# A streaming encoder layer on one core: the gate columns move into the index keys' weight tile, and the attention logits are fused with their row maximum

## The chip, the cores and the metric

The kernel runs on one core of one Trainium2 chip. A core has a matrix engine (TensorE, PE in the profile; its weight loads are shown as PEld), a vector engine (VectorE, DVE), a scalar engine (ScalarE, ACT), a general engine (GpSimd, POOL) and a queue that issues DMAs (SyncE, SP). The metric is the device time of one execution in microseconds; less is better.

## The reference, cut to what matters

One layer of a hybrid encoder is computed for 1024 prompt tokens and 8 x 16 sample tokens, 1152 in all, in float32: a half-step feed-forward block, a token mixer, a second feed-forward block, and a final norm. The change lies in the mixer:

```python
aq, ak, av, iq, ik, iw, mq, mk, mv, mif, mo, gates = jnp.split(h @ w_in, offs, axis=-1)
...
rel = jax.nn.relu(jnp.einsum('bqhd,bsd->bqhs', q_idx, k_idx))
score = jnp.einsum('bqhs,bqh->bqs', rel, w_idx) * IDX_SCALE       # 4 index heads
_, sel = lax.top_k(score, top_k)
...
logits = (jnp.einsum('bqhd,bqkd->bqhk', q, k_sel) * DH_A ** -0.5
          - alibi_slopes()[None, None, :, None] * dist[:, :, None, :])
p = jax.nn.softmax(logits, axis=-1)                               # 8 heads, 64 wide
```

`w_in` is 1024 x 4556. Its columns are, in order: 512 attention queries, 64 + 64 keys and values, 256 index queries, 64 index keys, 4 index weights, 1024 columns of mLSTM queries, keys and values, 8 mLSTM gates (`mif`), 512 output gates (`mo`), 2048 branch gates.

## The kernel before

The program is a row of phases with a barrier after each: `load_residual`, `ffn`, `project`, `prepare_mix`, `mlstm`, `mlstm_output`, `attention`, `output`, `ffn`, `final_norm`. Activations lie transposed, channels on the 128 partitions and tokens along the free dimension. Every float32 product is made of three in a reduced-precision format (`product3`): operands are split into a high part (ScalarE copies it) and a low part (GpSimd subtracts), and TensorE adds low x high, high x low and high x high.

**`project`** (`d_` tiles) multiplies the normed activations with `w_in` in tiles of 128 columns. A tile is 3 groups of 384 tokens x 8 blocks of 128 channels x 3 products, 72 matmuls of 384 columns. The list `COLS` gives the first nine tiles: two of index queries, one with index keys and index weights (`C_IK`, tile 2), four of attention queries, one of keys and values, and one that begins at the eight gate columns (`C_MI`, tile 8, `GATES`). Then come 8 tiles of mLSTM columns, which stay on chip (`mix`), and 20 that ScalarE puts through a sigmoid into `stage`, from where they are stored to DRAM. That is 37 tiles. `HEAD` is unrolled, `LOOP1` and `LOOP2` are hardware loops over two tiles each. For each tile `load` issues the DMA on SyncE, `split_hi` (ScalarE) and `split_lo` (GpSimd) make `d_w_hi` and `d_w_lo`, `unit` (TensorE) multiplies, `evict` (ScalarE) empties PSUM, `store` (SyncE) stores. Weight buffers are double (`n0 % 2`), and `load` runs one tile ahead.

Between tile 2 and tile 3 every engine runs `scores`: SyncE issues `copies()` (the index keys doubled to both halves of the partitions, six DMAs that count up `dup`, and others), ScalarE and VectorE split queries and keys, TensorE makes the index scores. Then VectorE runs the top-k selection alone (`max` and `match_replace` in turn), while TensorE goes on with tile 3 and the rest. The selection leaves in `DM`, for each query and key, the distance to the key, plus 1e30 where the key is not selected. The gates' tile is stored whole to DRAM (`sc_v[N_SIG]`), and `prepare_mix` reads its eight rows back.

**`attention`** (`t_` tiles) runs 52 items over 9 query tiles of 128 rows; query tile t sees (t + 1) x 128 keys, the sample tile 528. An item is 4 heads for the first two query tiles, 2 for the next two, and 1 for the rest. For an item i, TensorE makes `product(i)` into `t_ps_l`; VectorE makes `logits(i)` with one instruction for each head (distance x slope + product), one `reduce_max` over the item and one small multiply that gives the negated maximum `t_nm`; ScalarE's `probs(i)` takes the exponential with the row sum; VectorE's `normalise(i)` multiplies with the inverse sum; TensorE's `transposes(i)` turn the probabilities, ScalarE's `evict(i)` copies them, TensorE's `values(i)` multiply them with the values. The order of each engine's queue is written by hand. TensorE's is:

```python
                product(0)
                product(1)
                for i in range(len(ITEMS)):
                    if i + 2 < len(ITEMS):
                        product(i + 2)
                    transposes(i)
                    ...
                    if i:
                        values(i - 1)
```

and VectorE's is `logits(0)`, `logits(1)`, then `normalise(i)`, `logits(i + 2)` for each i. The queries of query tile t + 2 are split by ScalarE (`query_hi`) and GpSimd (`query_lo`) after the last item of query tile t.

Of the kernel before, what the change touches and what calls it, by code (L numbers as in the profile page):

```python
# [22 lines left out]
P = 128  # L23
# [12 lines left out]
HA = 8  # L36
# [14 lines left out]
SLOPE = [2.0 ** (-8.0 * (h + 1) / HA) / QK_SCALE for h in range(HA)]  # L51
# [18 lines left out]
def constants():  # L70
# [7 lines left out]
    c["slope"] = -np.repeat(np.array(SLOPE, np.float32), DEC_SEQ)[:, None]  # L78
# [490 lines left out]
def project(nc, ctx, M, K, io, out, xT, x_dram, xn_hi, xn_lo, aq, kvT, DM, mix, aq_at, kvT_at, mix_at, scratch):  # L569
# [13 lines left out]
    COLS = [C_IQ, C_IQ + P, C_IK, C_AQ, C_AQ + P, C_AQ + 2 * P, C_AQ + 3 * P, C_AK, C_MI]  # L583
    HEAD, LOOP1, MID, LOOP2, TAIL = range(9), (9, N_MIX // 2 - 1), range(15, 19), (19, N_SIG // 2 - 2), (35, 36)
    GATES, MIX, SIG = 8, 9, 17
    TILES = [7, 6, 5, 4, 3, 2, NTP]
    with ExitStack() as mem, M.scope():
# [18 lines left out]
        pair_mask = M.high("pair_mask_sb", [P, 4, P])  # L606
        k_lo = M.at("d_k_lo", [P, SEQ], M.low_end, F32R)
# [52 lines left out]
        with nc.Block() as block:  # L660
            @block.sync
            def _(sp):
                def load(i, n0):
                    if n0 >= 2:
                        sp.wait_ge(lo_ok, i * 2 + (n0 - 1))
                    if n0 < len(COLS):
                        src = w_v[:, :, COLS[n0]:COLS[n0] + P]
                    elif n0 < SIG:
                        src = w_v[:, :, bass.ds(i * (2 * P) + (C_MQ + (n0 - 9) * P), P)]
                    else:  # L670
                        src = w_v[:, :, bass.ds(i * (2 * P) + (C_MO + (n0 - 17) * P), P)]
                    sp.dma_start(raw[:, n0 % 2], src).then_inc(w_in[n0 % 2], 16)

                def store(i, n0):
                    if n0 != GATES and n0 < SIG:
                        return
                    sp.wait_ge(ev_ok, i * (2 * NCH) + NCH * (n0 + 1))
                    if n0 == GATES:
                        sp.dma_start(sc_v[N_SIG], stage[:, 0]).then_inc(gates_out, 16)
                        return  # L680
# [5 lines left out]
                def copies():  # L686
                    sp.wait_ge(ev_ok, 3 * NCH)
                    for half in range(2):
# [13 lines left out]
                def first():  # L702
# [4 lines left out]
                    for dst, n in ((dist_p, "dist_p"), (dist_s, "dist_s"), (pair_mask, "pair_mask")):  # L707
# [8 lines left out]
            def _(act):  # L716
                def split_hi(i, n0):
                    act.wait_ge(w_in[n0 % 2], i * 16 + 16 * (n0 // 2 + 1))
# [4 lines left out]
                def evict(i, n0):  # L723
                    if n0 == 3:
                        act.wait_ge(spilled, 16)
                    if n0 == MIX:
                        act.wait_ge(acc_ok, len(TILES) * NI)
                    if n0 == SIG:
# [3 lines left out]
                    for c in range(NCH):  # L732
# [15 lines left out]
                        nc.scalar.activation(dst, src, ACT.Sigmoid if n0 >= SIG else ACT.Copy)\  # L748
# [39 lines left out]
            def _(pe):  # L788
# [15 lines left out]
                def scores():  # L804
                    pe.wait_ge(ld, 16 * (DEC_BATCH + 3))
# [692 lines left out]
def attention(nc, ctx, M, K, io, E, DM, o_hi, o_lo):  # L1498
# [17 lines left out]
    with ExitStack() as mem, M.scope():  # L1516
# [9 lines left out]
        mx, nm, sm, inv = (M.low("t_" + n, [P, 2, 4]) for n in ("mx", "nm", "sm", "inv"))  # L1526
# [675 lines left out]
```

## Time and profile before

| what | value |
|---|---|
| median of 3 runs | 2839.64 us (2838.19 to 2847.57) |
| the profiled execution's own time | 2833.4 us |
| its span, first to last instruction | 2831.4 us |
| TensorE, VectorE, GpSimd, ScalarE busy | 95%, 42%, 26%, 25% of the span |
| mean granted TensorE clock | 0.965 |
| `project` | about 861 to 1407 us of the span |
| `attention` | about 1556 to 1753 us |

Times in the views are microseconds from the start of the span, unless marked ns. An engine counts as busy while an instruction runs on it; the number in brackets behind a timeline row is how long the engine was idle before it, and what ended that. Matmuls are pipelined, so the ends of matmuls overlap with the next starts: starts are the better measure. A few matmul records are missing from a trace.

### The profile page before, as it was taken

To read this page: it belongs to the slowest core of one execution; us is meant where nothing else is said; L and a number is where in the kernel's file an instruction comes from. 1 tells how busy PE (TensorE), PEld (TensorE's weight loads), DVE (VectorE), ACT (ScalarE), POOL (GpSimd) and SP (SyncE) were. 2 spreads that over 40 slices of the span, in tenths; PEclk is the share of its full clock that TensorE was granted. 3 is DMA by queue.
4 is the path that set the end of the run, shared out by engine and by line. 5 is a ranking of instruction groups with operands and counts; after the bars stand their busy time and mean duration, and the time that the engine had idled before them with its cause. 6 is when DMAs were issued, how large, how long until landed. Compare 5 with 4: busy or idle time off the path is not lost. (4 is left out here: it accounts for less than half of the span.)

```text
span 2831.4 us, 38415 instructions
## 1 busy us (share of the span) xinstructions
PE 2694.5 (95%) x15459; PEld 2605.1 (92%) x15459; DVE 1198.0 (42%) x2109; ACT 700.8 (25%) x1258; POOL 726.6 (26%) x396
## 2 busy tenths in 40 slices
PE   7999999999998899999886898998999999999998
PEld 7999999999997599999864686998999999999998
DVE  5122222222234699999644785423222222222226
ACT  5111111111124311211163774112311111111112
POOL 5222222222214012111221311422522222222221
PEclk9999999999999899999976899998999999999999
DMA  4111111111103111132312201331111111111101
GB/s 129 44 45 45 45 45 33 43 45 45 45 1 127 39 46 45 55 95 90 86 41 51 46 1 57 122 135 45 53 45 45 31 45 45 45 45 42 33 30 75
DMA packets 193642, 154.50 MB, mean 55 GB/s; under 512 B 32292, under 2 KB 178128, under 8 KB 193244
## 3 DMA queue, kind: packets, MB, share of 16 engines
q1 hardware_dynamic: 193500, 152.45, 18.2%
q8 instruction: 109, 1.79, 0.3%
q14 instruction: 33, 0.27, 0.0%
HBM read 124.56 MB, written 23.90 MB: 52 GB/s over the span
## 5 line engine op out<-in xcount | busy, mean ns | idle before, releaser
L356 PE MATMUL f1ps_up<-xn_lo,f1w_hi 128*128 128x384 f32 x1056 | 354.3, 335 | 8.3 <-POOL xn_lo L311 8.3
L356 PE MATMUL f2ps_up<-xn_lo,f2w_hi 128*128 128x384 f32 x1056 | 354.0, 335 | 5.3 <-POOL xn_lo L311 5.2
L357 PE MATMUL f1ps_up<-xn_hi,f1w_lo 128*128 128x384 f32 x1056 | 353.8, 335 | 0.0
L358 PE MATMUL f1ps_up<-xn_hi,f1w_hi 128*128 128x384 f32 x1056 | 353.7, 335 | 0.0
L357 PE MATMUL f2ps_up<-xn_hi,f2w_lo 128*128 128x384 f32 x1056 | 353.3, 335 | 0.0
L358 PE MATMUL f2ps_up<-xn_hi,f2w_hi 128*128 128x384 f32 x1056 | 353.3, 335 | 0.0
L356 PE MATMUL d_ps<-xn_lo,d_w_hi 128*128 128x384 f32 x888 | 299.3, 337 | 7.5 <-POOL xn_lo L311 5.8
L357 PE MATMUL d_ps<-xn_hi,d_w_lo 128*128 128x384 f32 x888 | 298.1, 336 | 0.0
L358 PE MATMUL d_ps<-xn_hi,d_w_hi 128*128 128x384 f32 x888 | 298.0, 336 | 0.0
L514 DVE TENSOR_TENSOR f1hid<-f1gate,f1ps_up 128x384 f32<-128x384 f32 x66 | 36.6, 554 | 503.2 <-ACT f1gate L483 503.2
L514 DVE TENSOR_TENSOR f2hid<-f2gate,f2ps_up 128x384 f32<-128x384 f32 x66 | 36.6, 554 | 503.1 <-ACT f2gate L483 503.1
L435 POOL TENSOR_TENSOR f2w_lo<-f2raw,f2w_hi 128x2048 fp32r<-128x2048 f32 x33 | 152.1, 4608 | 217.7 <-ACT f2w_hi L431 217.7
L356 PEld LDWEIGHTS f1ps_up<-xn_lo,f1w_hi 128*128 128x128 f32 x1056 | 199.0, 188 | 9.7 <-issue 9.4
L783 POOL TENSOR_TENSOR d_w_lo<-d_raw,d_w_hi 128x1024 fp32r<-128x1024 f32 x37 | 89.1, 2408 | 459.7 <-ACT d_w_hi L721 459.6
L435 POOL TENSOR_TENSOR f1w_lo<-f1raw,f1w_hi 128x2048 fp32r<-128x2048 f32 x33 | 152.0, 4607 | 213.2 <-ACT f1w_hi L431 213.2
L356 PEld LDWEIGHTS f2ps_up<-xn_lo,f2w_hi 128*128 128x128 f32 x1056 | 198.7, 188 | 6.9 <-issue 6.7
L357 PEld LDWEIGHTS f1ps_up<-xn_hi,f1w_lo 128*128 128x128 f32 x1056 | 199.1, 189 | 0.1
L358 PEld LDWEIGHTS f1ps_up<-xn_hi,f1w_hi 128*128 128x128 f32 x1056 | 199.1, 188 | 0.0
L357 PEld LDWEIGHTS f2ps_up<-xn_hi,f2w_lo 128*128 128x128 f32 x1056 | 198.8, 188 | 0.1
L358 PEld LDWEIGHTS f2ps_up<-xn_hi,f2w_hi 128*128 128x128 f32 x1056 | 198.6, 188 | 0.0
L522 DVE SCALAR_TENSOR_TENSOR xT<-f2ps_dn,xT 128x384 f32<-128x384 f32 x264 | 147.2, 558 | 113.7 <-PE f2ps_dn L358 113.4
L522 DVE SCALAR_TENSOR_TENSOR xT<-f1ps_dn,xT 128x384 f32<-128x384 f32 x264 | 147.2, 558 | 113.7 <-PE f1ps_dn L358 113.4
(302 smaller groups left out, 5402.5 us busy)
## 6 DMA issues: line engine op xcount, KB each, us to landing
f1raw<-in_w_ffn_up SPq DMA_DIRECT2D x44, 512.0 KB
f2raw<-in_w_ffn_up SPq DMA_DIRECT2D x44, 512.0 KB
d_raw<-in_w_in SPq DMA_DIRECT2D x37, 512.0 KB, 4.1
p_dram<-stage SPq DMA_DIRECT2D x21, 576.0 KB, 3.1
f1raw<-in_w_ffn_down SPq DMA_DIRECT2D x11, 1024.0 KB
f2raw<-in_w_ffn_down SPq DMA_DIRECT2D x11, 1024.0 KB
b_sg<-p_dram SPq DMA_DIRECT2D x16, 576.0 KB, 4.9
x_dram<-xT SPq DMA_DIRECT2D x1, 4608.0 KB, 15.1
```

The source lines that it names most:

```text
L356: nc.tensor.matmul(out, w_hi, x_lo, start=first, stop=False)
L357: nc.tensor.matmul(out, w_lo, x_hi, start=False, stop=False)
L358: return nc.tensor.matmul(out, w_hi, x_hi, start=False, stop=final)
L435: nc.gpsimd.tensor_tensor(slot(w_lo, n0), slot(raw, n0), slot(w_hi, n0).bitcast(F32), ALU.subtract).then_inc(lo_ok, 1)
L514: nc.vector.tensor_tensor(hid[:, q0 % 2], gate[:, q0 % 2], ps_up[:, c, 1, 0:CH], ALU.mult).then_inc(hid_ok, 1)
L522: nc.vector.scalar_tensor_tensor(x, ps_dn[:, r % 2, 0:CH], 0.5, x, ALU.mult, ALU.add).then_inc(dn_ev, 1)
L783: nc.gpsimd.tensor_tensor(w_lo[:, n0 % 2], raw[:, n0 % 2], w_hi[:, n0 % 2].bitcast(F32), ALU.subtract).then_inc(lo_ok, 1)
```

## The change

Two edits. First, the gates' tile is gone: `COLS` has eight entries, and tile 2 (`INDEX`) is loaded by two DMAs, 96 columns from the index keys on and 32 columns from the gates on, so that the gates come out in rows 96 to 103 of `ikw`. They are stored from there, in front of the copies of the index keys; ScalarE's wait for that store is now at the first `mix` tile. 36 tiles are left, and all tile numbers behind the eighth move down by one. Second, ScalarE's eviction of the attention queries scales them by -1/8 / slope of their head (`qscale`, a new constant that is loaded with the others), so that (distance + product) x slope is the negated logit; one tensor_tensor_reduce for each head writes it together with its minimum over the keys, which is `t_nm`. The reduce over the item, the small multiply and two semaphores go; the exponential takes scale -1.

```diff
-SLOPE = [2.0 ** (-8.0 * (h + 1) / HA) / QK_SCALE for h in range(HA)]
+SLOPE = [2.0 ** (-8.0 * (h + 1) / HA) for h in range(HA)]
...
-    c["slope"] = -np.repeat(np.array(SLOPE, np.float32), DEC_SEQ)[:, None]
+    c["slope"] = np.repeat(np.array(SLOPE, np.float32), DEC_SEQ)[:, None]
+    c["qscale"] = -QK_SCALE / np.repeat(np.array(SLOPE, np.float32).reshape(4, 2).T, DH, axis=0)
...
-    COLS = [C_IQ, C_IQ + P, C_IK, C_AQ, C_AQ + P, C_AQ + 2 * P, C_AQ + 3 * P, C_AK, C_MI]
-    HEAD, LOOP1, MID, LOOP2, TAIL = range(9), (9, N_MIX // 2 - 1), range(15, 19), (19, N_SIG // 2 - 2), (35, 36)
-    GATES, MIX, SIG = 8, 9, 17
+    COLS = [C_IQ, C_IQ + P, C_IK, C_AQ, C_AQ + P, C_AQ + 2 * P, C_AQ + 3 * P, C_AK]
+    HEAD, LOOP1, MID, LOOP2, TAIL = range(8), (8, N_MIX // 2 - 1), range(14, 18), (18, N_SIG // 2 - 2), (34, 35)
+    INDEX, MIX, SIG, G_ROW = 2, 8, 16, 96
...
                 def load(i, n0):
                     if n0 >= 2:
                         sp.wait_ge(lo_ok, i * 2 + (n0 - 1))
+                    if n0 == INDEX:
+                        sp.dma_start(raw[:, 0, :, 0:G_ROW], w_v[:, :, C_IK:C_IK + G_ROW]).then_inc(w_in[0], 16)
+                        sp.dma_start(raw[:, 0, :, G_ROW:P], w_v[:, :, C_MI:C_MI + P - G_ROW]).then_inc(w_in[0], 16)
+                        return
...
                     sp.wait_ge(ev_ok, i * (2 * NCH) + NCH * (n0 + 1))
-                    if n0 == GATES:
-                        sp.dma_start(sc_v[N_SIG], stage[:, 0]).then_inc(gates_out, 16)
-                        return
...
                 def copies():
                     sp.wait_ge(ev_ok, 3 * NCH)
+                    sp.dma_start(sc_v[N_SIG, 0:2 * HM], ikw[G_ROW:G_ROW + 2 * HM, :]).then_inc(gates_out, 16)
...
-                    for dst, n in ((dist_p, "dist_p"), (dist_s, "dist_s"), (pair_mask, "pair_mask")):
+                    for dst, n in ((dist_p, "dist_p"), (dist_s, "dist_s"), (pair_mask, "pair_mask"),
+                                   (qscale, "qscale")):
...
-                    act.wait_ge(w_in[n0 % 2], i * 16 + 16 * (n0 // 2 + 1))
+                    act.wait_ge(w_in[n0 % 2], i * 16 + 16 * (n0 // 2 + 1 + (n0 >= INDEX and n0 % 2 == 0)))
...
                     if n0 == 3:
                         act.wait_ge(spilled, 16)
+                        act.wait_ge(ld, 16 * (DEC_BATCH + 4))
                     if n0 == MIX:
                         act.wait_ge(acc_ok, len(TILES) * NI)
-                    if n0 == SIG:
                         act.wait_ge(gates_out, 16)
...
-                        nc.scalar.activation(dst, src, ACT.Sigmoid if n0 >= SIG else ACT.Copy)\
+                        nc.scalar.activation(dst, src, ACT.Sigmoid if n0 >= SIG else ACT.Copy,
+                                             scale=qscale[:, n0 - 3:n0 - 2] if 3 <= n0 < 7 else 1.0)\
                             .then_inc(ev_ok, 1)
...
-                    pe.wait_ge(ld, 16 * (DEC_BATCH + 3))
+                    pe.wait_ge(ld, 16 * (DEC_BATCH + 4))
...
                         if t < NTP:
-                            dist, by = DM[:, SCORE_OFF[t]:SCORE_OFF[t] + L], -SLOPE[x]
+                            dist, by = DM[:, SCORE_OFF[t]:SCORE_OFF[t] + L], SLOPE[x]
...
-                        last = v.scalar_tensor_tensor(heads(lg, i)[:, y], dist, by, ps_l[:, i % 2, base:base + L],
-                                                      ALU.mult, ALU.add)
+                        last = v.tensor_tensor_reduce(heads(lg, i)[:, y], dist, ps_l[:, i % 2, base:base + L], by,
+                                                      -TAKEN, ALU.add, ALU.min, nm[:, i % 2, y:y + 1])
                     last.then_inc(lg_ok, 1)
-                    dve.wait_ge(lg_ok, i + 1)
-                    v.reduce_max(mx[:, i % 2, 0:g], heads(lg, i), AX_X).then_inc(mx_ok, 1)
-                    dve.wait_ge(mx_ok, i + 1)
-                    v.tensor_scalar(nm[:, i % 2, 0:g], mx[:, i % 2, 0:g], -QK_SCALE, None, ALU.mult)\
-                        .then_inc(nm_ok, 1)
...
-                    act.wait_ge(nm_ok, i + 1)
+                    act.wait_ge(lg_ok, i + 1)
...
-                                                    bias=nm[:, i % 2, y:y + 1], scale=QK_SCALE,
+                                                    bias=nm[:, i % 2, y:y + 1], scale=-1.0,
```

## Rows read from the trace of the kernel before

**Rows 1.** The page, busy time of each engine.
```profile
PE 2694.5 (95%) x15459; PEld 2605.1 (92%) x15459; DVE 1198.0 (42%) x2109; ACT 700.8 (25%) x1258; POOL 726.6 (26%) x396
```

**Rows 2.** Windows, tiles 3 to 36: PE, PEld, DVE, ACT, POOL busy, clock, DMA share, GB/s.
```profile
978.70:1402.80 424.10, 424.10 (x2448) 424.10 (x2448) 393.25 (x649) 82.94 (x136) 79.56 (x33) 1.00 0.22 67
```

**Rows 3.** Timeline (start, duration), both ends of the projection behind the scores.
```profile
978.57 0.42 PE L356 MATMUL d_ps<-xn_lo,d_w_hi 128*128 128x384 f32 x1
...
1385.37 2.79 DVE L930 TENSOR_TENSOR DM<-DM,dist_s_sb 128x528 f32<-128x528 f32 x1
...
1402.81 0.34 PE L358 MATMUL d_ps<-xn_hi,d_w_hi 128*128 128x384 f32 x1
1406.91 2.16 PE L1124 MATMUL e_ps<-ident_sb,kvT 128*128 128x128 f32 x9 [3.76 <-PEq L660]
```

**Rows 4.** DMA issues from 855 to 960: count, KB each, median us to landing.
```profile
d_raw<-in_w_in SPq DMA_DIRECT2D x6, 512.0 KB, 4.8
iqm<-in_cache_idx_k SPq DMA_DIRECT2D x8, 128.0 KB, 5.2
```

**Rows 5.** Timeline, the head of the projection.
```profile
880.61 1.05 SPq L672 DMA_DIRECT2D d_raw<-in_w_in  x2
...
890.79 4.91 POOL L783 TENSOR_TENSOR d_w_lo<-d_raw,d_w_hi 128x1024 fp32r<-128x1024 f32 x2
...
892.17 1.05 ACT L721 ACTIVATE d_w_hi<-d_raw 128x1024 fp32r<-128x1024 f32 x1
...
906.38 1.05 ACT L721 ACTIVATE d_w_hi<-d_raw 128x1024 fp32r<-128x1024 f32 x1
...
925.51 1.06 ACT L763 ACTIVATE d_k_hi<-ikd 128x1024 fp32r<-128x1024 f32 x1 [4.72 <-DMA iqd<-iq]
...
929.51 1.22 DVE L879 TENSOR_TENSOR d_k_lo<-ikd,d_k_hi 128x1024 fp32r<-128x1024 f32 x1
```

**Rows 6.** Windows, the attention's query tile with 1024 keys; columns as in rows 2.
```profile
1686.80:1717.80 31.00, 30.81 (x217) 25.27 (x215) 27.85 (x41) 20.62 (x40) 2.32 (x3) 1.00 0.01 1
```

**Rows 7.** Groups by form, attention, VectorE: busy us, mean ns, idle before.
```profile
L1701 DVE SCALAR_TENSOR_TENSOR t_lg<-DM,t_ps_l 128x1024 f32<-128x1024 f32 x8 | 9.8, 1221 | 2.6 <-PE t_ps_l L1632 2.5
L1705 DVE TENSOR_REDUCE t_mx<-t_lg 128x1 f32<-128x1024 f32 x8 | 9.8, 1220 | 0.3
...
L1701 DVE SCALAR_TENSOR_TENSOR t_lg<-DM,t_ps_l 128x128 f32<-128x128 f32 x8 | 1.8, 281 | 4.7 <-PE t_ps_l L1632 4.7
```

**Rows 8.** Groups by line, attention, VectorE; shapes of a line taken together.
```profile
L1705 DVE TENSOR_REDUCE t_mx<-t_lg 128x1 f32<-128x640 f32 (+8 forms) x52 | 50.8, 976 | 1.8
...
L1707 DVE TENSOR_SCALAR t_nm<-t_mx 128x1 f32<-128x1 f32 (+2 forms) x52 | 8.7, 166 | 1.8
```

**Rows 9.** Waits of TensorE, 1577.5 to 1751: us in total, times, longest.
```profile
PE t_ps_t L1647 <- DVE t_p L1719: 2.7, 6, 0.8
PE t_ps_t L1647 <- DVE t_p L1717: 0.7, 3, 0.3
...
PEld t_ps_t L1647 <- DVE t_p L1719: 4.9, 7, 1.2
PEld t_ps_t L1647 <- DVE t_p L1717: 4.4, 16, 0.6
```

**Rows 10.** Timeline, TensorE, two items: 512 keys, then 1024 keys.
```profile
1605.40 0.40 PE L1632 MATMUL t_ps_l<-t_k_lo,t_qs 128*128 128x512 f32 x1
1606.60 1.09 PE L1647 MATMUL t_ps_t<-ident_sb,t_p 128*128 128x128 f32 x8 [0.79 <-DVE t_p L1719]
...
1713.28 0.39 PE L1632 MATMUL t_ps_l<-t_k_lo,t_qs 128*128 128x512 f32 x1
1713.51 1.03 PE L1647 MATMUL t_ps_t<-ident_sb,t_p 128*128 128x128 f32 x8
```

**Rows 11.** Timeline, from the second item's normalisation to the third query tile.
```profile
1570.40 0.69 DVE L1719 TENSOR_TENSOR t_p<-t_p,t_inv 128x512 f32<-128x512 f32 x1
...
1577.81 0.66 PE L1631 MATMUL t_ps_l<-t_k_hi,t_qs 128*128 128x384 f32 x1 [4.99 <-POOL t_qs L1590]
```

More of the change, by code:

```diff
@@ L606, in project @@
         pair_mask = M.high("pair_mask_sb", [P, 4, P])
+        qscale = M.low("qscale", [P, 4])
         k_lo = M.at("d_k_lo", [P, SEQ], M.low_end, F32R)
@@ L668, in load @@
                     elif n0 < SIG:
-                        src = w_v[:, :, bass.ds(i * (2 * P) + (C_MQ + (n0 - 9) * P), P)]
+                        src = w_v[:, :, bass.ds(i * (2 * P) + (C_MQ + (n0 - MIX) * P), P)]
                     else:
-                        src = w_v[:, :, bass.ds(i * (2 * P) + (C_MO + (n0 - 17) * P), P)]
+                        src = w_v[:, :, bass.ds(i * (2 * P) + (C_MO + (n0 - SIG) * P), P)]
                     sp.dma_start(raw[:, n0 % 2], src).then_inc(w_in[n0 % 2], 16)
                 def store(i, n0):
-                    if n0 != GATES and n0 < SIG:
+                    if n0 < SIG:
                         return
                     sp.wait_ge(ev_ok, i * (2 * NCH) + NCH * (n0 + 1))
-                    if n0 == GATES:
-                        sp.dma_start(sc_v[N_SIG], stage[:, 0]).then_inc(gates_out, 16)
-                        return
                     tile = i * 2 + (n0 - SIG)
@@ L1525, in attention @@
         k_lo = M.at("t_k_lo", [P, SEQ], E["kvT_at"], F32R)
-        mx, nm, sm, inv = (M.low("t_" + n, [P, 2, 4]) for n in ("mx", "nm", "sm", "inv"))
+        nm, sm, inv = (M.low("t_" + n, [P, 2, 4]) for n in ("nm", "sm", "inv"))
         ofs = M.low("t_ofs", [P, 2, 2 * P])
@@ L1530, in attention @@
         ps_o = psum(nc, mem, "t_ps_o", [P, HA, P])
-        (ld, ldm, qk, lg_ok, mx_ok, nm_ok, p_ok, inv_ok, pn_ok, tr, tr_ev, pv, of_ok, hi, lo,
+        (ld, ldm, qk, lg_ok, p_ok, inv_ok, pn_ok, tr, tr_ev, pv, of_ok, hi, lo,
          kh_ok, kl_ok, qh_ok, ql_ok) = (
-            sem(n) for n in ("ld", "ldm", "qk", "lg_ok", "mx_ok", "nm_ok", "p_ok", "inv_ok", "pn_ok", "tr",
+            sem(n) for n in ("ld", "ldm", "qk", "lg_ok", "p_ok", "inv_ok", "pn_ok", "tr",
                              "tr_ev", "pv", "of_ok", "hi", "lo", "kh_ok", "kl_ok", "qh_ok", "ql_ok"))
```

## The prediction

> **What bounds the kernel now.** I read the page first for the share of each engine: TensorE is busy 2694.5 us of a span of 2831.4 us, 95%, and VectorE, the next one, 42% [rows 1]. That is only an average, so I went on to the two stages that the change touches and asked in each which wait ends last.
>
> The first stage is the projection. After the indexer's scores TensorE runs its remaining 34 weight tiles without a gap: the window from 978.7 to 1402.8 has 424.10 us of TensorE busy in 424.10 us, at a granted clock of 1.00, while VectorE, which does the top-k selection meanwhile, is busy 393.25 us [rows 2]. The timeline gives the two ends: the first matmul starts at 978.57, the last at 1402.81, and the next phase starts at 1406.91, when the last eviction, its store and the barrier are through [rows 3]. VectorE's last instruction of the phase ends at 1385.37 + 2.79 = 1388.16 [rows 3]. So TensorE sets the end of this stage, and VectorE is 14.6 us earlier.
>
> The second stage is the attention (1561 to 1751). With 1024 keys TensorE is busy 30.81 of 31.00 us and VectorE 27.85 [rows 6]. Each engine waits for the other in turn, and since TensorE's queue is in order, the time that counts is what TensorE loses in front of its transposes, where it waits for the normalised probabilities `t_p` of VectorE [rows 9].
>
> **The change, part by part. The weight tile.** The eight gate columns no longer have a tile of their own. A tile is 3 column groups x 8 blocks x 3 products = 72 matmuls. From rows 3: (1402.81 - 978.57) / (34 x 72 - 1) = 0.1733 us from start to start, so a tile is 72 x 0.1733 = 12.48 us. The loops keep their lengths (3, 8 bodies of two tiles); one unrolled tile of the head goes. Gone with it are a 512 KB load, its ScalarE split and its GpSimd split, three evictions and a 576 KB store, all of which ran beside the matmuls: I count them at nothing, since TensorE has no gap there that they could have filled [rows 2]. The sum of this part is -12.5 us, if the stage stays TensorE's.
>
> Does it? The last matmul then starts at 1390.3, and the next phase could start at 1406.91 - 12.48 = 1394.4. VectorE's selection does not depend on the tiles behind the scores and ends at 1388.16 as before: its margin shrinks from 18.7 to 6.2 us. It is not used up unless the selection starts over 6 us late. What could delay it lies in front of the scores, and is the next part.
>
> **Packing and the moved store.** Tile 2 is now loaded in two pieces, 96 and 32 columns, so 384 and 128 bytes per row instead of 512, twice as many pieces (2048). The issue is the second of two at 880.61, so about 881.1; ScalarE splits that tile at 892.17; at 906.38 ScalarE splits tile 3, for which it waits until tile 1 is multiplied, so TensorE begins tile 2 at about 906.3 [rows 5]. Bounds for the landing: 4.8 us, as the whole tiles of that stretch, or four times the 5.2 us of a key cache load, which has 512 pieces of 256 bytes [rows 4], so 20.8 us. At the low end nothing moves. At the high end the tile lands at 902, its splits take 1.05 us on ScalarE and 2.4 on GpSimd [rows 5], and it is there at 905.4, still before 906.3. I take the low end, and 0 us; being later than that would cost its lateness one for one. The constant `qscale` (2 KB) adds one short issue in front of the load of tile 1, hidden by the same margin, and TensorE's wait for one more load at the scores is long met. The gate store is now issued from the index keys' tile in front of the six copies that feed `d_k_hi`: one issue more, bounded by 0 and 0.6 us (two issues took 1.05 us [rows 5]). ScalarE starts `d_k_hi` at 925.51, so it ends at 926.6, but VectorE takes up `d_k_lo` only at 929.51 because of its own queue [rows 5]: 2.9 us of cover, so 0. The load of tile 4 behind them is needed only after 978. ScalarE's wait for the constants in front of tile 3 lies behind the scores and is met; behind it in its queue are only evictions. The scale of the query eviction becomes an operand of an instruction that was there.
>
> **The fused logits.** 72 scalar_tensor_tensor instructions become 72 tensor_tensor_reduce, and 52 reduces and 52 small multiplies go: 50.8 + 8.7 = 59.5 us of VectorE [rows 8], among them two waits of VectorE on itself per item. The trace has no such fused instruction. Nearest are the unfused one on the same operands, 1221 ns for 1024 columns and 281 ns for 128, thus (1221 - 281) / 896 = 1.049 ns a column and 147 ns fixed, and the reduce at 1220 ns [rows 7]. Lower bound: as the unfused one. Upper bound: both in a row, 2.44 us, two passes, which leaves VectorE where it was. I take one pass plus a readout of the row minimum like the small multiply, at most 166 ns [rows 8], because both present instructions run at the same rate for a column.
>
> The Trainium skill (VectorE: DVE Perf Modes, section Two Vector instructions with no wait between them) has it that an instruction which also writes out its accumulator is two, the main one and a read of the accumulator; no row of VectorE shows this here, and it would not change the sum.
>
> What is that worth? VectorE's removed time is not the gain; TensorE's lost time is. Where nothing holds it, a transpose starts 0.23 us after the last 512-column matmul (1713.28 to 1713.51); in the fourth query tile it is 1.20 us (1605.40 to 1606.60), thus 0.97 lost [rows 10]. Reading all 48 items from the third query tile on in this way gives 0.9 us in the third, 2.8 in the fourth, 1.8 in the next four and 0.5 in the sample tile: 6.0 us. The waits' view bounds it: 2.7 + 0.7 = 3.4 us by matmuls, 4.9 + 4.4 = 9.3 by weight loads [rows 9]. Without the reduce VectorE needs about 1.3 us less per item at 1024 keys, far more than is lost anywhere, so most of it should go; TensorE is next, and ScalarE's exponentials and copies, which stand in one queue, may keep some. I take 4.6 of the 6.0.
>
> In front of that TensorE waits for the third tile's query split, which hangs on VectorE: item 1's normalisation starts at 1570.40, then come its transposes, their eviction, the query's two splits, and the product at 1577.81 [rows 11]. Three items' logits lie before 1570.40. The first saves nothing (item 1's product is only just ready). The second saves a reduce of 512 columns (147 + 512 x 1.049 = 684 ns) and 0.17, the third 1.22 and 0.17, together 2.2 us; eight readouts at some 0.1 us, since small instructions overlap, take back 0.8. That leaves 1.4 us (0 to 2.2).
>
> **Sum.** -12.5 - 4.6 - 1.4 = -18.5 us. The profiled execution took 2833.4 us itself (its span and 2.0 around it) and would take 2814.9. The median of the runs shown is 2839.64, 6.2 us above it; the same difference gives 2821.1.
>
> **Rivals.** *A, the tile alone pays:* the fused instruction needs two passes, and VectorE keeps its load; attention gains at most 1 us. For it: no row shows the fused instruction. Against it: the unfused one reads the same two operands at 1.049 ns a column. -12.5 - 0.5 = -13 gives 2826.6. The Trainium skill (Vector Engine (DVE) Microarchitecture Reference, section Points that are easy to get wrong) says that a two-source instruction with accumulation and two non-bf16 SBUF sources runs at half throughput. Here one source is PSUM; should it hold all the same, it is this rival. Chance 0.14.
>
> *B, the head or the selection holds the tile's gain back:* tile 2 lands late, or the selection slips by over 6.2 us. A wait of x us at tile 2 moves scores, selection and end by x. It would have to land over 906.3 - 881.1 - 3.4 = 21.8 us after its issue, more than four times what the whole tiles take [rows 4]. With 5 us lost: -13.5, 2826; with 10 lost, 2831. The Trainium skill (DMA: Bandwidth & Descriptors, section Specifications) wants at least 512 B per transfer for full rate, so by it the pieces are slower; at half rate, by an estimate, they land within 10 us, hidden. Chance 0.05.
>
> *C, slower than before:* the fused instruction streams at several passes. All items have 8 x 4608 + 8 x 528 = 41088 columns, so each further pass costs 41088 x 1.049 ns = 43.1 us of VectorE, against 59.5 removed. In the tile of 1024 keys two further passes cost 2 x 8.6 us, the reduces and multiplies give back 11.0, and 3.1 us idle [rows 6] absorb half of the rest: 3 us longer in 31. That tile has a fifth of all columns, and the others have more idle time, so attention would be some 10 us longer, and the total -2.5, no change. It turns slower just beyond three passes; at four, 10 + 43 us longer in attention, -12.5 + 53 gives 2880. Against it: no two-source row is slower than one pass. Chance 0.03.
>
> *D, more gain:* all 9.3 us of the weight loads' waits and 2.2 at the start go: -24, 2815.6. Chance 0.04. The forecast, with a gain of 15 to 23, has 0.74.
>
> **Range and chances.** 2815 to 2829: D's end below, A's above with some 2 us for the median of a few runs that lie 9 us apart. For the forecast alone 2816.5 to 2825. A measurement of this kernel can tell about 0.3%, 8.5 us, from no change. Forecast, A, D and half of B are faster by more: 0.93. Same 0.04 (the other half of B, and C near three passes). Slower 0.03.
>
> **What the profile after should show.** 2592 instead of 2664 matmuls on `d_ps`, 36 weight splits; from the last score to the last matmul 33 x 12.48 = 411.8 us without a gap; the weight load of tile 2 landing before 892; VectorE's selection ending about 6 us before the next phase begins; the fused row at 1.2 to 1.4 us for 1024 columns and no reduce; VectorE in the 1024-key tile about 18 instead of 28 us busy of some 31; waits of the transposes for `t_p` near 1 us; the third tile's first product about 1.4 us nearer to the phase's first. The forecast is wrong if the fused row is over 2 us, if TensorE's gap before the transposes moves to ScalarE or to another place of its queue, or if TensorE waits at tile 2.

## The result, and the profile after

The kernel with the change takes 2820.76 us (median of 5 runs, 2818.27 to 2823.03) beside 2839.64 us (5 runs) for the kernel before: ratio 0.9936, 95% interval 0.992 to 0.9952, 18.9 us less. 2821.1 was forecast. The profiled execution took 2819.09 us itself, with a span of 2817.3 us, 14.1 less than that of before; the forecast for it was 2814.9. So the median agrees while the profile misses 4.2 us, and the parts have to be taken one at a time.

The page's busy times; [rows 1] are those of before:

```profile
PE 2683.2 (95%) x15387; PEld 2597.3 (92%) x15387; DVE 1138.7 (40%) x2077; ACT 696.5 (25%) x1254; POOL 721.3 (26%) x395
```

VectorE has 59.3 us less work and TensorE 72 matmuls fewer. The 59.5 counted for VectorE are met partly by chance: in the attention its busy time falls by 57.5 us (154.0 to 96.6), for the row minima are now read out by an instruction of their own, and 2.1 us come from one add at the end of the selection, seen below. The timeline of both ends of the projection behind the scores, beside [rows 3]:

```profile
979.47 0.42 PE L357 MATMUL d_ps<-xn_lo,d_w_hi 128*128 128x384 f32 x1
...
1386.25 0.71 DVE L936 TENSOR_TENSOR DM<-DM,dist_s_sb 128x528 f32<-128x528 f32 x1
...
1394.39 0.33 PE L359 MATMUL d_ps<-xn_hi,d_w_hi 128*128 128x384 f32 x1
...
1398.59 2.15 PE L1130 MATMUL e_ps<-ident_sb,kvT 128*128 128x128 f32 x9 [3.87 <-PEq L662]
```

The next phase starts 8.3 us earlier, not 12.5. The selection ends at 1386.96 and leaves 11.6 us, so it is not what holds the stage. From the first matmul to the last are 414.92 us for 33 tiles, 0.1747 us a matmul instead of 0.1733. Windows of 300 us of before, then of after (columns as in [rows 2]):

```profile
1000.00:1300.00 300.00, 300.00 (x1732) 300.00 (x1731) 289.66 (x438) 59.61 (x98) 57.69 (x24) 1.00 0.21 63
```

```profile
1000.00:1300.00 300.00, 300.00 (x1719) 300.00 (x1719) 289.70 (x438) 59.05 (x96) 55.35 (x23) 1.00 0.21 63
```

Both are busy all the time at a granted clock of 1.00, and still one does 1732 matmuls and the other 1719. A busy share can't show this; the count can.

The DMA issues of the head, from 855 to 925, and the timeline of the queue:

```profile
d_raw<-in_w_in SPq DMA_DIRECT2D x1, 384.0 KB, 5.6
...
d_raw<-in_w_in SPq DMA_DIRECT2D x1, 128.0 KB, 6.2
```

```profile
880.51 0.74 SPq L669 DMA_DIRECT2D d_raw<-in_w_in  x1
881.29 2.98 SPq L670 DMA_DIRECT2D d_raw<-in_w_in  x1
...
891.17 1.05 ACT L726 ACTIVATE d_w_hi<-d_raw 128x1024 fp32r<-128x1024 f32 x1
```

Tile 2's second piece lands at 881.29 + 6.2 = 887.5, before the 892 that was asked for, and ScalarE splits it without a wait.

VectorE in the attention, by form, beside [rows 7] and [rows 8]:

```profile
L1707 DVE CUSTOM_DVE_ANT_0 t_lg<-DM,t_ps_l 128x1024 f32<-128x1024 f32 x8 | 9.8, 1222 | 13.4 <-PE t_ps_l L1638 13.4
...
L1707 DVE DVE_READ_ACCUMULATOR2_ANT t_nm<- 128x1 f32 x72 | 5.9, 83 | 0.0
...
L1707 DVE CUSTOM_DVE_ANT_0 t_lg<-DM,t_ps_l 128x128 f32<-128x128 f32 x8 | 1.8, 284 | 5.5 <-PE t_ps_l L1638 5.5
```

The fused instruction takes 1222 ns for 1024 columns, the unfused one took 1221: one pass. The row minimum comes out in an instruction of its own of 83 ns. The Trainium skill (VectorE: DVE Perf Modes, section Two Vector instructions with no wait between them) says that such an instruction is two, and these rows agree. TensorE's waits, 1567 to 1735, beside [rows 9]:

```profile
PE t_ps_t L1653 <- DVE t_p L1720: 0.6, 1, 0.6
```

```profile
PEld t_ps_t L1653 <- DVE t_p L1720: 1.1, 1, 1.1
...
PEld t_ps_t L1653 <- DVE t_p L1718: 0.2, 1, 0.2
```

What was 3.4 us in 9 waits of the matmuls is 0.6 us in one. In the windows, a stretch of 31 us at the tile of 1024 keys shows VectorE at 16.40 us, where it was 27.85 in [rows 6]:

```profile
1669.50:1700.50 31.00, 31.00 (x221) 26.10 (x219) 16.40 (x32) 20.48 (x40) 1.97 (x3) 1.00 0.01 1
```

Last, the start of the attention in the timeline, beside [rows 11]: first product, item 1's normalisation, GpSimd's split, third query tile, and the phase's last values:

```profile
1552.22 0.45 PE L1637 MATMUL t_ps_l<-t_k_hi,t_qs 128*128 128x128 f32 x1 [8.79 <-POOL t_qs L1596]
...
1559.29 0.69 DVE L1720 TENSOR_TENSOR t_p<-t_p,t_inv 128x512 f32<-128x512 f32 x1
...
1563.27 2.65 POOL L1596 TENSOR_TENSOR t_qs<-aq,t_qs 64x512 fp32r<-64x512 f32 x2 [8.43 <-ACT t_qs L1777]
...
1566.06 0.66 PE L1637 MATMUL t_ps_l<-t_k_hi,t_qs 128*128 128x384 f32 x1 [3.65 <-POOL t_qs L1596]
...
1733.28 0.43 PE L1673 MATMUL t_ps_o<-t_pt,vn 16*64 16x128 f32 x2
```

The third tile starts 13.84 us behind the first product; before it was 1577.81 - 1561.10 = 16.71. From the first product to the last values are 181.06 us; before, with these rows, 189.28:

```profile
1561.10 0.44 PE L1631 MATMUL t_ps_l<-t_k_hi,t_qs 128*128 128x128 f32 x1 [8.80 <-POOL t_qs L1590]
...
1573.99 1.22 DVE L1719 TENSOR_TENSOR t_p<-t_p,t_inv 128x1024 f32<-128x1024 f32 x1
1574.12 3.54 POOL L1590 TENSOR_TENSOR t_qs<-aq,t_qs 64x512 fp32r<-64x512 f32 x2 [10.42 <-ACT t_qs L1776]
...
1750.38 0.43 PE L1667 MATMUL t_ps_o<-t_pt,vn 16*64 16x128 f32 x2
```

The open points: why the matmuls are slower, why the attention gives 8.2 us and not 6.0, and where the profile's remaining 8.3 + 8.2 - 14.1 = 2.4 us went (the span is only 14.1 us shorter).

### The profile page after: what moved, and what is told of

Read it like the earlier page. It is cut to its first block and busy times, and to the rows that moved or that the text cites. A ratio compares the mean times of both kernels' runs of the same rounds, so it can differ in the third digit from the quotient of the medians.

```text
span 2817.3 us, 38246 instructions
## 1 busy us (share of the span) xinstructions
PE 2683.2 (95%) x15387; PEld 2597.3 (92%) x15387; DVE 1138.7 (40%) x2077; ACT 696.5 (25%) x1254; POOL 721.3 (26%) x395
## 5 line engine op out<-in xcount | busy, mean ns | idle before, releaser
L357 PE MATMUL d_ps<-xn_lo,d_w_hi 128*128 128x384 f32 x864 | 293.1, 339 | 6.3 <-POOL xn_lo L312 4.7
L358 PE MATMUL d_ps<-xn_hi,d_w_lo 128*128 128x384 f32 x864 | 291.8, 338 | 0.0
L359 PE MATMUL d_ps<-xn_hi,d_w_hi 128*128 128x384 f32 x864 | 291.6, 338 | 0.0
L436 POOL TENSOR_TENSOR f2w_lo<-f2raw,f2w_hi 128x2048 fp32r<-128x2048 f32 x33 | 152.1, 4608 | 217.8 <-ACT f2w_hi L432 217.8
L436 POOL TENSOR_TENSOR f1w_lo<-f1raw,f1w_hi 128x2048 fp32r<-128x2048 f32 x33 | 152.0, 4606 | 212.9 <-ACT f1w_hi L432 212.9
```

The lines of the kernel that those rows point to most:

```text
L357: nc.tensor.matmul(out, w_hi, x_lo, start=first, stop=False)
L358: nc.tensor.matmul(out, w_lo, x_hi, start=False, stop=False)
L359: return nc.tensor.matmul(out, w_hi, x_hi, start=False, stop=final)
L436: nc.gpsimd.tensor_tensor(slot(w_lo, n0), slot(raw, n0), slot(w_hi, n0).bitcast(F32), ALU.subtract).then_inc(lo_ok, 1)
```

## The experiments

*Tiles* is the time from the first to the last start of a projection matmul behind the scores, *attention* that from the first product to the last values, and *clock* TensorE's mean granted clock in the 10 us from the third query tile's first product on.

**The two parts alone, and both kernels again.** The first two are the change without the one part or without the other:

```diff
 # e1_tile_only: the logits as before
+                        last = v.scalar_tensor_tensor(heads(lg, i)[:, y], dist, by, ps_l[:, i % 2, base:base + L],
+                                                      ALU.mult, ALU.add)
...
+                    v.reduce_max(mx[:, i % 2, 0:g], heads(lg, i), AX_X).then_inc(mx_ok, 1)
 # e2_fuse_only: the tiles as before
+    COLS = [C_IQ, C_IQ + P, C_IK, C_AQ, C_AQ + P, C_AQ + 2 * P, C_AQ + 3 * P, C_AK, C_MI]
```

> The packed tile alone: 36 weight tiles, logits and maximum as before. By the prediction the projection gives 12.5 us and nothing else moves, so about 2827 on the median. The rival from the profile after is that the shorter kernel runs its projection matmuls 0.8% slower (0.1747 us from start to start instead of 0.1733): then the phase behind the projection starts only 8 to 9 us earlier, about 2831. The start-to-start time of the matmuls behind the scores decides: 0.1733 or 0.1747.

> The fused logits alone: 37 weight tiles as before. By the prediction the attention gives 6.0 us (4.6 in front of the transposes, 1.4 at its start), about 2833.6 on the median. By the profile after it gives 8.2 us between the first product and the last values (2.9 of them at the start), about 2831.4. The matmuls of the projection should keep 0.1733 us from start to start if the slower rate belongs to the packed tile; if they show 0.1747 here as well, the rate belongs to the execution and not to the change.

> The changed kernel once more, nothing edited. If the slower matmul rate belongs to the kernel, the 33 tiles behind the scores take 415 us again (0.1747 us from start to start). If it belongs to the execution, another value comes out, 0.1733 as likely as any. Attention from first product to last values 181.1 us again, within 0.3.

> The kernel before once more, nothing edited. If its rate belongs to the kernel, the 34 tiles behind the scores take 424.2 us again (0.1733 us from start to start); if it varies from execution to execution, up to 427.6 (0.1747). Attention from first product to last values 189.3 us again, within 0.3.

Measured: e1 2828.56 us beside 2837.99 (ratio 0.9967, 0.9953 to 0.9981), e2 2830.47 (0.997, 0.9953 to 0.9986). The tile alone gives 9.4 us and the fused logits 7.5, about the whole together. In the profiles:

| kernel | tiles | us a matmul | attention | clock |
|---|---|---|---|---|
| before; e4, the same | 424.24; 424.23 (34) | 0.1733 | 189.28; 189.22 | 0.85; 0.86 |
| after | 414.92 (33) | 0.1747 | 181.06 | 0.73 |
| e3, as after | 419.67 (33) | 0.1767 | 179.84 | 0.85 |
| e1, tile only | 414.93 (33) | 0.1747 | 190.32 | 0.69 |
| e2, fused only | 432.39 (34) | 0.1767 | 180.99 | 0.74 |

The same program has 0.1747 in one execution and 0.1767 in the next, and e2, with its 37 tiles, has 0.1767. So the packed tile is not needed for the slow rate. The spread of the attention has another source, the last column. Before the third tile TensorE stands idle, for 5.0 us with the old logits and for 3.6 to 4.2 with the new, and around the tile's start its granted clock falls to the lower of its two levels. In some executions it stays there longer than in others, and the attention is then 1.1 to 1.2 us longer with the same queues. The windows of before, e1 and after (PE, PEld, DVE, ACT, POOL, clock):

```profile
1577.80:1587.80 10.00, 9.82 (x60) 8.52 (x61) 7.35 (x14) 7.21 (x18) 2.38 (x3) 0.85 0.25 55
```

```profile
1571.90:1581.90 10.00, 9.96 (x52) 8.85 (x53) 6.60 (x12) 6.24 (x15) 1.27 (x2) 0.69 0.24 52
```

```profile
1566.10:1576.10 10.00, 10.00 (x56) 8.83 (x56) 4.55 (x13) 6.64 (x16) 1.70 (x2) 0.73 0.23 50
```

So like has to be compared with like: 189.25 with 179.84 us where the clock came back early (before and e4; e3), 190.32 with 181.0 where it came back late (e1; after and e2). Either way the fused logits give 9.3 to 9.4 us; the pair of before and after mixes the two and shows 8.2.

Back to the rate. e3's window counts 1700 matmuls, at the same granted clock of 1.00:

```profile
1000.00:1300.00 300.00, 300.00 (x1700) 300.00 (x1699) 289.78 (x434) 58.75 (x95) 55.33 (x23) 1.00 0.21 61
```

**The reduce put back.** The item's reduce runs again behind the fused instructions, and ScalarE waits for it:

```diff
-                    last.then_inc(lg_ok, 1)
+                    last.then_inc(fu_ok, 1)
+                    dve.wait_ge(fu_ok, i + 1)
+                    v.reduce_max(mx[:, i % 2, 0:g], heads(lg, i), AX_X).then_inc(lg_ok, 1)
```

> The changed kernel with a reduce over the item put back behind the fused instructions, and ScalarE waiting for it; its result is not used. VectorE has the load of before less the 8.7 us of small multiplies. If the attention's gain is VectorE's removed time, it goes: first product to last values 188 to 189.3 us again instead of 181.1, of which 2.2 at the start. This is also what rival A (two passes) would have been: a total 6 to 8 us above the changed kernel. If the gain came from the fewer semaphore waits and the missing small multiply, attention stays below 184.

Measured: 2825.64 us beside 2838.84 (0.995, 0.9933 to 0.9966), attention 186.27. VectorE's groups by line in it:

```profile
L1711 DVE TENSOR_REDUCE t_mx<-t_lg 128x1 f32<-128x640 f32 (+8 forms) x52 | 50.8, 976 | 1.8
L1707 DVE CUSTOM_DVE_ANT_0 t_lg<-DM,t_ps_l 128x128 f32<-128x128 f32 (+7 forms) x64 | 46.7, 752 | 24.8 <-PE t_ps_l L1638 22.7 <-ACT t_p L1743 1.9
```

Neither of the two outcomes named. The clock as defined above is 0.71 here, so the profiles to compare are e1 (190.32) and after (181.06): the 50.8 us of reduces cost 5.2 of the 9.3 us, and the small multiply (8.7 us) with its wait, less the readouts that came in, the other 4.1. This holds in this order only: no run takes the reduces away and leaves the multiplies. Summed item by item as in the prediction, TensorE's loss before the transposes is 2.7 us here, 6.0 before and 0.9 after. That fits a loss that is only what lies beyond each item's slack: 0.17 us less on VectorE's path in every item took 3.3 us off it, and some 1 us less took 1.8. This reading is argued, not tried.

**Four passes.** Every fused instruction is issued four times, each after the end of the one before:

```diff
+                        for again in range(4):
+                            if again:
+                                dve.wait_ge(fu_ok, passes)
                             last = v.tensor_tensor_reduce(heads(lg, i)[:, y], dist, ps_l[:, i % 2, base:base + L], by,
                                                           -TAKEN, ALU.add, ALU.min, nm[:, i % 2, y:y + 1])
```

> The changed kernel with every fused instruction issued four times in a row, each after the one before has ended, which is an instruction of four passes (rival C of the prediction). By its working attention is 53 us longer than that of before, 242 us from the first product to the last values, and the whole is near 2880. If TensorE's time hid more of VectorE's than the working says, it is under 225; if the waits between the passes count, over 250.

Measured: 2918.83 us (one run), attention 278.23. The window of the attention (PE, PEld, DVE, ACT, POOL):

```profile
1554.80:1833.40 278.60, 200.88 (x1208) 159.43 (x1208) 258.30 (x680) 132.16 (x309) 31.15 (x31) 0.89 0.04 9
```

VectorE is the bound now, 258 of 279 us, and TensorE, busy for 201 of them, is granted 0.89. The sign of rival C's working is right and its size 36 us short (242 forecast). 216 further instructions at 1.049 ns a column are 3 x 43.1 = 129 us, but each also has the 147 ns fixed cost from [rows 7], 32 us more, which the working left out. Rival C was one instruction of four passes with one fixed cost, so this run is somewhat dearer than what it stands for.

**Tile 2 in seven pieces.** Smaller pieces, to find how far the load is from being late. ScalarE's wait for them is counted up to match:

```diff
-                        sp.dma_start(raw[:, 0, :, 0:G_ROW], w_v[:, :, C_IK:C_IK + G_ROW]).then_inc(w_in[0], 16)
+                        for c0 in range(0, G_ROW, 16):
+                            sp.dma_start(raw[:, 0, :, c0:c0 + 16], w_v[:, :, C_IK + c0:C_IK + c0 + 16]).then_inc(w_in[0], 16)
```

> The changed kernel with the 96 columns of tile 2 loaded by six DMAs of 16 columns (64 bytes a row), and the gates' 32 as before: seven issues and 7168 pieces instead of 2048. By the prediction only a landing later than 21.8 us after the issue costs anything, one for one. If a piece has a price of its own, as the 6.2 us of the 32-column piece with 1024 rows suggest, the seven land 20 to 45 us after 881, TensorE waits at tile 2 for up to 25 us, and the selection and the end move with it. If bytes set the time, it lands within 10 us and nothing moves but five issues of 0.5 to 0.8 us.

Measured: 2822.88 us (one run); tiles 411.75 us, attention 180.08. The DMA issues and the queue:

```profile
d_raw<-in_w_in SPq DMA_DIRECT2D x6, 64.0 KB, 3.1
...
d_raw<-in_w_in SPq DMA_DIRECT2D x1, 128.0 KB, 3.6
```

```profile
880.42 7.53 SPq L670 DMA_DIRECT2D d_raw<-in_w_in  x6
887.99 1.06 SPq L671 DMA_DIRECT2D d_raw<-in_w_in  x1
...
891.62 1.06 ACT L727 ACTIVATE d_w_hi<-d_raw 128x1024 fp32r<-128x1024 f32 x1 [0.52 <-DMA d_raw<-in_w_in]
```

Seven times 1024 pieces are in by 891.6, 11 us after the first issue, and the issues (7.53 us for six) take longer than the transfers behind them. ScalarE waits half a microsecond, and TensorE not at all: the landing 20 to 45 us after 881 was wrong. Rival B needs a landing later than 21.8 us after the issue, and even these pieces are far from it. This run also has the matmuls at 0.1733, with the packed tile.

**The third tile's queries split earlier.** In ScalarE's queue the split goes before item 0's eviction:

```diff
                         probs(i + 1)
+                    if i == 0:
+                        query_hi(2)
                     evict(i)
-                    if t + 2 < NTP and i + 1 == FIRST[t + 1]:
+                    if 0 < t and t + 2 < NTP and i + 1 == FIRST[t + 1]:
```

> The changed kernel with ScalarE's split of the third tile's queries one place earlier in its queue, before the eviction of item 0 instead of behind that of item 1. If the start of attention hangs on this split, as the prediction says, GpSimd takes it up 2 to 3 us earlier, and the third tile's first product comes 11 to 11.8 us after the phase's first product instead of 13.8; the total falls by 2 to 3 us. If something else is as late there (item 0's eviction now comes 1.3 us later, and the logits of item 2 behind it), less than 1 us comes out.

Measured: 2813.41 us beside 2838.84 (0.9907, 0.9891 to 0.9923), attention 175.82. The timeline:

```profile
1549.50 0.44 PE L1637 MATMUL t_ps_l<-t_k_hi,t_qs 128*128 128x128 f32 x1 [8.80 <-POOL t_qs L1596]
...
1557.04 2.72 POOL L1596 TENSOR_TENSOR t_qs<-aq,t_qs 64x512 fp32r<-64x512 f32 x2 [4.93 <-ACT t_qs L1777]
...
1559.90 0.41 PE L1637 MATMUL t_ps_l<-t_k_hi,t_qs 128*128 128x384 f32 x1 [0.18 <-POOL t_qs L1596]
```

The third tile starts 10.40 us behind the first product, with a gap of 0.18 us for TensorE instead of 3.65. Another 1.8 us come from the rest of the attention (165.42 us instead of 167.22), and it goes with the granted clock of the 10 us behind the third tile's start: in e8 and e10, with next to no gap, it is 1.00, and the rest takes 165.4 and 164.9 us; with the gap it is 0.85 and 0.83 in e3 and e7 (166.1 and 166.3 us) and 0.72 to 0.74 in the other four profiles of these logits (167.1 to 167.3).

**A control, a further version, and the selection left out.** e9 is the changed kernel again. e10 is e8 with the first tile's low parts made by VectorE:

```diff
-                query_lo(0, 0)
...
+                dve.wait_ge(qh_ok, 2)
+                for r in range(2):
+                    q, q_hi, q_lo = query_parts(0, r)
+                    v.tensor_tensor(q_lo, q, q_hi.bitcast(F32), ALU.subtract).then_inc(ql_ok, 1)
```

e11 leaves out all but one round of the selection: `for _ in range(1)` instead of `range(full)`.

> The changed kernel a third time, as the control on the same chip for the versions sent with it: near 2821 on the median. Matmuls behind the scores from start to start at one of the three values seen so far (0.1733, 0.1747 or 0.1767 us), whichever; attention 180 to 181 us, the third tile's first product 13.7 to 13.8 us behind the phase's first.

> The version with the early query split of the third tile, and in it VectorE instead of GpSimd makes the low parts of the first tile's queries, behind the keys' low part. GpSimd needs 2.6 us for the two from ScalarE's last split on, VectorE some 0.6 to 0.7 us each, starting when the keys' low part ends: the phase's first product comes 1.0 to 1.5 us earlier, and the total is 1 to 1.5 us below the version with the early split alone, 7 to 9 us below the changed kernel (of it 3.4 from the earlier split and 1 to 2 from a clock that does not fall in the gap). If GpSimd's split of the second tile's queries, which then runs beside VectorE, becomes the late one, nothing is gained over the early split alone.

> The changed kernel with one round of eight maxima instead of all the rounds in the top-k selection, so that it leaves out nearly all of the selection (the attention works on other distances, with the same instructions). If the selection sets nothing, the next phase starts 4.2 us behind the last projection matmul as before, and nothing before it moves: 2817 to 2826. If the slower matmuls behind the scores come from VectorE's selection running beside them, this run must show 0.1733 us from start to start; if it shows 0.1747 or 0.1767, the selection is not the cause.

Measured: e9 2820.94 us beside 2839.16 (0.993, 0.9905 to 0.9956), e10 2816.23 (0.9913, 0.9895 to 0.9931), e11 2812.51 (one run). e10's first product comes 3.89 us after the start of the keys' split, 5.05 in the changed kernel, and its attention takes 175.28 us. That is 1.2 us less than in the changed kernel for the first, and for the second 0.5 less than in e8, but its median is no lower than e8's, so whether it helps the whole stays open. Tiles: e9 414.92, e10 419.67, e11 411.75 us. In e11 the selection is over at 1008 instead of 1387, and the next phase still starts 4.20 us behind the last projection matmul, so the selection set nothing. About the rate e11 tells nothing: it has 0.1733, but so have e6 and e7 with the whole selection.

**The kernel before a third time.**

> The kernel before a third time, to see whether its projection matmuls, too, can take one of the slower rates that six profiles of the changed kernel and its variants showed (0.1747 or 0.1767 us from start to start). If the rate belongs to the execution, 424.2 us, 427.6 or 432.4 for the 34 tiles behind the scores, any of them; if the kernel before is free of it, 424.2 a third time. Attention 189.2 us again.

Measured: tiles 427.50 us for 34, 0.1747 us each, attention 190.40, time 2840.97 us (one run). (The profiles with a slower rate up to then were eight, not six.) Its window:

```profile
1000.00:1300.00 300.00, 300.00 (x1720) 300.00 (x1719) 289.67 (x439) 58.65 (x96) 55.24 (x23) 1.00 0.21 63
```

So the kernel before takes the middle rate as well. The level belongs to the execution. The attention's 190.40 us go with a clock of 0.69 in the 10 us behind the third tile's first product, as in e1.

## Why the prediction was right, and where it was not

**The tile, right in size.** At each of the three rates there is a kernel with 34 tiles and one with 33 behind the scores: 424.24 and 411.75, 427.50 and 414.92, 432.39 and 419.67 us. The differences are 12.5, 12.6 and 12.7 us, and the forecast's 33 x 12.48 = 411.8 us is what e6, e7 and e11 show. The profile after fell on the middle rate, the profile before on the fast one; that took 33 x 72 x 1.33 ns = 3.2 us from the 12.5. The step was right, its check against one pair of profiles misled. Another 0.9 us went in front of the tiles, where the first matmul behind the scores came later (979.47 against 978.57): from the phase's first matmul to it are 118.9 us in after and e1, 117.0 in before and e4, but 118.7 in e12, and 116.7 to 117.7 in e2 and the eight other packed runs, so that is the execution too.

**Packing, the moved store, the scale: nothing, as forecast.** The low bound held for the landing (6.2 us against 4.8), and e7 shows the high one far away. The margin of the selection is 11.6 us, not 6.2: the next phase starts 4.2 us later than forecast, and the selection ends 1.2 us earlier. Its last add, the same instruction in both profiles, took 2.79 us before, beside GpSimd's split of a weight tile, and 0.71 after.

**The fused instruction: one pass, as forecast,** and rival A with C fell with it. The readout was bounded by 166 ns and is 83. The Trainium skill (Vector Engine (DVE) Microarchitecture Reference, section Points that are easy to get wrong) gives half throughput for two-source accumulation with both sources in SBUF. With one of them in PSUM the instruction took 1222 ns for 1024 columns, no more than the unfused one, so the rule does not reach this form. No run here has both in SBUF, so the rule itself is neither borne out nor refuted.

**The attention: right in mechanism, too small in size.** 6.0 us was the sum (4.6 + 1.4); the profile gives 8.2, and 9.3 at like clock. Over all profiles, four with the old logits (189.2 to 190.4) and six with the new and otherwise unchanged queues (179.8 to 181.2), the means are 189.8 and 180.7 us, a gain of 9.1. Two terms were mis-sized. *The start* was 1.4 and is 2.9 in every pair (16.7 before, 13.7 to 13.9 after). Item 1's normalisation comes 2.2 us earlier, for the readouts that were to take back 0.8 us run in the shadow of the next instruction: four fused instructions of 128 columns start 0.21 us apart. Another 0.6 lies behind it: the step there, GpSimd's query split, takes 2.65 us instead of 3.54, and the normalisation of item 2 on VectorE, which ran beside it before, is nearly over when it starts: 1573.99 + 1.22 is 1575.21, and from there two splits of 1.27 us end at 1577.75, where the row has 1577.66. The first of these two splits takes 2.21 us in all four profiles with the old logits and 1.26 to 1.35 in the six with the new ones. e5 tries it, though it was not made for it: the reduce moves the normalisation back beside the split, and the split takes 2.06 us again (the row has both splits):

```profile
1569.39 1.23 DVE L1722 TENSOR_TENSOR t_p<-t_p,t_inv 128x1024 f32<-128x1024 f32 x1
...
1569.68 3.40 POOL L1596 TENSOR_TENSOR t_qs<-aq,t_qs 64x512 fp32r<-64x512 f32 x2 [10.08 <-ACT t_qs L1779]
```

*The loss before the transposes* was to fall by 4.6 of 6.0 and fell by 5.1; nothing moved to ScalarE. Of the remaining 1.3 of 9.3 us, e12 beside after shows some 1.1 between the first transposes and the values of an item, in many small amounts. Rival D's bounds for the same two terms were 9.3 and 2.2, so the truth lies between forecast and D.

**What was not in the sum.** 12.5 + 9.1 = 21.6 us, and the medians differ by 18.9. The interval of that difference is 13.6 to 22.7 us, so the times alone do not show that anything is missing. The profiles do, in two stages that the change does not touch.

*Between the projection and the attention.* From the start of the next phase to the attention's first product the same instructions take 154.2 to 154.5 us in the three profiles of the kernel before and 155.5 in e2, but 152.0 to 163.2 in the ten with the packed tile, 157.3 in the mean. Two of these, e7 and e11, in the windows (PE, PEld, DVE, ACT, POOL, clock):

```profile
1393.70:1556.90 163.20, 112.67 (x545) 86.48 (x546) 75.24 (x156) 71.49 (x210) 35.24 (x27) 0.62 0.25 53
```

```profile
1394.10:1546.10 152.00, 101.33 (x546) 77.20 (x546) 75.20 (x156) 71.28 (x210) 35.31 (x28) 0.68 0.26 57
```

The other engines do the same work, TensorE's takes 11.3 us longer, and the granted clock is 0.62 instead of 0.68. TensorE pauses often in this stage, and how long it is at the lower of its two levels (1.2 and 2.4 GHz) differs from run to run. Over all fourteen profiles the stage's length goes with it: 152.0 and 152.2 us at 0.68, 153.6 to 155.5 at 0.66 and 0.67, 156.6 and 156.8 at 0.64, 159.6 to 163.2 at 0.62. Whether the packed tile makes the low values more frequent, or ten profiles against four had bad luck, stays open.

*Behind the attention.* The tail (from the output phase's first matmul to the end) took 1071.0 to 1072.7 us in the three of before, 1072.2 in e2, and 1073.4 to 1074.3 in nine of the ten packed ones. One part of this does belong to the packed tile. The output phase loads the residual back from DRAM (4608 KB), VectorE's add waits for it, and TensorE for the add. Before, then after:

```profile
1862.63 0.34 SPq L1865 DMA_DIRECT2D xT<-x_dram  x1
...
1876.17 1.49 DVE L1954 TENSOR_TENSOR xT<-b_ps,xT 128x384 f32<-128x384 f32 x3 [11.84 <-DMA xT<-x_dram]
```

```profile
1846.13 0.34 SPq L1866 DMA_DIRECT2D xT<-x_dram  x1
...
1861.28 1.49 DVE L1955 TENSOR_TENSOR xT<-b_ps,xT 128x384 f32<-128x384 f32 x3 [13.46 <-DMA xT<-x_dram]
```

The output phase's matmuls behind that add, by form, before and then after:

```profile
L356 PE MATMUL b_ps<-y_lo,b_w_hi 128*128 128x384 f32 x192 | 64.2, 334 | 1.8 <-DVE xT L1954 1.8
```

```profile
L357 PE MATMUL b_ps<-y_lo,b_w_hi 128*128 128x384 f32 x192 | 64.8, 338 | 3.4 <-DVE xT L1955 3.4
```

From the issue to the add are 13.5 to 13.6 us in all four profiles with 37 tiles, e2 among them, and 14.8 to 15.2 in all ten with 36. TensorE waits 1.8 to 1.9 us in the four and 3.0 to 3.4 in the ten. So this wait costs the packed kernels some 1.3 us, in e1 too, which has the old logits. Why the same load is slower there, no run shows. In the profile after, the tail with the step to it took 3.0 us more and the stage before the attention 0.6 less; that is the 2.4 us.

So the median agrees to 0.3 us by luck. The attention's gain was taken 3 us too small, and these stages, taken as unchanged, gave about as much back. The chances hold one slip: forecast, A, D and half of B add up to 0.945, not 0.93.

## What to carry to other kernels

Cost a reduce or a small operation by what the waiting engine loses behind it, item by item, and count the small one with its wait: here 8.7 us of multiplies, taken away first, were worth 4.1 us of the end and 50.8 us of reduces, taken away next, 5.2. Before believing a difference of a few microseconds between two profiles, profile the same kernel again and compare stage by stage, with the granted clock beside each stage; counts of matmuls in equal windows show what busy shares hide. And once an engine is relieved, look at the first wait that is left: one line moved in ScalarE's queue gave another 5 us of attention (e8).

## What the runs showed of the hardware

TensorE's matmuls of 384 columns in the projection run at 0.1733, 0.1747 or 0.1767 us from start to start, constant behind the scores within an execution, changing between executions of the same program, at a granted clock of 1.00, while the feed-forward phases of the same executions keep the fast rate. Of fourteen profiles five show the fast, five the middle and four the slow one. The delay is spread over all of them: at the fast rate every start follows the last by 173 or 174 ns, at the middle one by 170 to 178, at the slow one by 175 to 178. The cause is not found. A VectorE add of 528 columns took 0.71 us alone and 2.78 to 2.82 us in the three runs where a GpSimd split ran beside it; each time it ended 0.57 us after the split. The other way round, a GpSimd query split began over 0.1 us before the end of a VectorE normalisation in 35 cases over the fourteen profiles, and each time it ended 1.12 to 1.15 us after the normalisation, whether that was a tensor_tensor or a tensor_scalar; beside a reduce it took 1.27 to 1.28 us, as alone. The Trainium skill (SBUF — State Buffer, section Summary: rules for kernel authors) says that when VectorE has two SBUF inputs and GpSimd reads SBUF, the second to issue is blocked until the first is done, and that is what the add's rows and the splits' look like. In e11 the add's are:

```profile
1004.97 2.40 POOL L789 TENSOR_TENSOR d_w_lo<-d_raw,d_w_hi 128x1024 fp32r<-128x1024 f32 x1 [10.08 <-ACT d_w_hi L726]
...
1005.12 2.82 DVE L936 TENSOR_TENSOR DM<-DM,dist_s_sb 128x528 f32<-128x528 f32 x1
```

The accumulator's readout on VectorE takes 83 ns and is hidden behind the next instruction. ScalarE's eviction of 384 columns takes 583 ns with a scale from memory and 492 without, in the changed kernel by tile:

```profile
L753 ACT ACTIVATE aq<-d_ps,qscale x12: 581/583/588, 984.0 to 1030.1; 128x384 f32<-128x384 f32 x12
...
L753 ACT ACTIVATE kvT<-d_ps x3: 492/492/492, 1034.2 to 1042.6; 128x384 f32<-128x384 f32 x3
```
